# Attention value products of two heads in alternation by key tile, and the second head's probabilities scaled on GpSimd

## The chip, the cores and the metric

The kernel runs on one core of a Trainium2 chip. The time is the device time of one launch, in microseconds; the time of the kernel before is the median of three runs, 3374.5 us.

## The reference, cut to what matters

Two layers over 256 latent tokens and 256 context tokens, 1024 wide, in float32. In each layer an adaLN-modulated RMSNorm and one input projection feed three token mixers; their outputs are gated, merged and projected, and a product-key expert layer (128 picks for each token, gathered from memory) follows. The change lies in the three mixers alone:

```python
# A: 8 query heads on 2 key heads, window of 128, a sink logit;  B: 8 heads, 2-D neighbourhood, bias table
# C: 4 heads of two score maps each (differential attention)
p = softmax(concat([s_loc, s_ctx, sink]))        # A
p = softmax(concat([s + bias, s_ctx]))           # B
a = softmax(s0) - lam * softmax(s1)              # C
o = p @ v
```

Latent tokens read 512 keys (256 latent, 256 context), context tokens read the 256 context keys. The second layer has latent tokens alone.

## The kernel before, in words

The kernel is written with one program for each engine and semaphores between them. The attention of a layer is a list of steps, `STEPS[l]` (L66). A step is one stream `s` (0 latent, 1 context), one unit `u` of two heads (0 to 3 are mixer A, 4 to 7 mixer B, 8 to 11 mixer C) and one tile `qt` of 128 queries: 48 steps in layer 0 (24 latent, then 24 context) and 24 in layer 1 (latent). A latent step of A or B works on two heads (`m` = 0, 1) by 512 keys, a context step on two heads by 256 keys. `a` counts the steps over both layers. Four engines work on neighbouring steps at the same time:

- **TensorE** (`attention`, L675 to L741) goes through scores of step n+2 (L689, L692), transposes of the probabilities of step n (L704: eight 128x128 tiles, four for each head, in PSUM banks 4 and 5), then the value products of step n-1 (L726: for each head one accumulation over four key tiles, head 0 into PSUM partitions 0 to 63 and head 1 into 64 to 127 of one bank). In the float32 type each product is two instructions in the trace.
- **VectorE** (`maxima`, `normalise`, `copy_y`, L1438 to L1496) goes through the mask or bias of step i+1 (L1457), its row maxima (L1458, L1460 to L1462), the sums and reciprocals of step i (L1471, L1472), the scaling of its probabilities (L1475 head 0, L1476 head 1; mixer C has L1478 and L1479 in their place), and the copy of the output of step i-2 (L1486).
- **ScalarE** (L1044 to L1078) takes the exponentials of step i+1 (L1057, L1059) and copies the transposed probabilities of step i out of PSUM (L1071).
- **GpSimd** computes nothing here. It issues the bias tables of mixer B from memory (`biases`, L1236 to L1245), 256 KB for each of the 8 latent steps of B in a layer, into two buffers: table b goes where table b-2 was. The first two of a layer are issued ahead of the attention; table b from the third on waits for `max_ready` of the step that used table b-2, and is thus issued as soon as the row maxima of that step are done:

```python
if b % 8 >= 2:
    back = [k for k, v in BIASED.items() if v == b - 2][0]
    pool.wait_ge(max_ready, back + 1)
```

The order that matters on VectorE is that of L1489 to L1494: `maxima(i + 1)` stands ahead of `normalise(i)`, and its first instruction, L1457, waits for the scores and, in mixer B, for the bias table (L1455). Outside the attention GpSimd issues the gathers of the expert rows, with waits of their own.

Of the kernel before, what the change touches and what calls it, by code (L numbers as in the profile page):

```python
# [12 lines left out]
N_CTX = 256  # L13
T = N_LAT + N_CTX
TT = T // P
DEPTH = 2
# [50 lines left out]
STEP0 = [0, len(STEPS[0])]  # L67
# [105 lines left out]
def build(nc, x_in, small_in, lambda_in, const_in_dram, rope_in, bias_in, stream_in, experts_in, out):  # L173
# [8 lines left out]
    with ctx:  # L182
# [171 lines left out]
        max_ready = sem("max_ready")  # L354
        exp_ready = sem("exp_ready")
        prob_ready = sem("prob_ready")
        probt_done = sem("probt_done")
        probt_copied = sem("probt_copied")
        y_done = sem("y_done")
# [101 lines left out]
        def key_bank(r, n):  # L461

            return 4 + n % 4 if r == 1 else 2 + n % 6

        block = ctx.enter_context(nc.Block())

# [40 lines left out]
        def _(pe):  # L507
# [167 lines left out]
            def attention(l):  # L675
                steps = STEPS[l]

                def scores(n):
                    _, s, u, qt = steps[n]
                    a = STEP0[l] + n  # L680
                    q = UNIT_AT[("abc"[u // 4] + "q", u % 4)]
                    k = UNIT_AT[("abc"[u // 4] + "k", 0 if u < 4 else u % 4)]
                    if n >= 2:
                        pe.wait_ge(exp_ready, a - 1)
                    for m in range(2):
                        rows64 = slice(64 * m, 64 * m + 64)
                        query = feature(l, s, q)[rows64, qt * P:(qt + 1) * P]
                        if l == 0 and s == 0:
                            last = mm(ps[:, 2 * (a % 2) + m, :], query, feat0[rows64, k, :], start=True, stop=True)  # L689
                            continue  # L690
                        for at, ks in enumerate([0, 1] if s == 0 else [1]):
                            last = mm(ps[:, 2 * (a % 2) + m, at * N_LAT:(at + 1) * N_LAT], query,  # L692
                                      feature(l, ks, k)[rows64, :], start=True, stop=True)
                    last.then_inc(scores_done, 1)

                def transposes(n):
                    _, s, u, qt = steps[n]
                    a = STEP0[l] + n
                    pe.wait_ge(prob_ready, a + 1)
                    if a >= 1:  # L700
                        pe.wait_ge(probt_copied, a)
                    for m in range(2 if u < 8 else 1):
                        for t in range(TT if s == 0 else 2):
                            last = nc.tensor.transpose(ps[:, 4 + m, t * P:(t + 1) * P],  # L704
                                                       prob_l[l][:, a % 2, m, t * P:(t + 1) * P], ident)
                    last.then_inc(probt_done, 1)

                def values(n):
                    _, s, u, qt = steps[n]
                    a = STEP0[l] + n  # L710
                    nt = TT if s == 0 else 2
                    pe.wait_ge(probt_copied, a + 1)
                    if a >= 2:
                        pe.wait_ge(y_copied, a - 1)
                    y = ps[:, 6 + a % 2, 0:P]
                    for m in range(2 if u < 8 else 1):
                        for t in range(nt):
                            tile = TT - nt + t
                            if u < 4:
                                v, at = value_tile(l, 0, tile)[:, 64 * m:64 * m + 64], slice(64 * m, 64 * m + 64)  # L720
                            elif u < 8:
                                c0 = 128 * (u - 4) + 64 * m
                                v, at = value_tile(l, 1, tile)[:, c0:c0 + 64], slice(64 * m, 64 * m + 64)
                            else:
                                v, at = value_tile(l, 2, tile)[:, 128 * (u - 8):128 * (u - 7)], slice(0, 128)
                            last = mm(y[at, :], v, probt_l[l][:, a % 2, m, t * P:(t + 1) * P],  # L726
                                      start=(t == 0), stop=(t == nt - 1))
                    last.then_inc(y_done, 1)

                pe.wait_ge(proj_copied, PROJ0[3] if l else PROJ0[1])  # L730
                pe.wait_ge(roped, (l + 1) * len(ROPED))
                pe.wait_ge(v_copied, V0[3] if l else V0[1])
                scores(0)
                scores(1)
                for n in range(len(steps)):
                    if n + 2 < len(steps):
                        scores(n + 2)
                    transposes(n)
                    if n >= 1:
                        values(n - 1)  # L740
                values(len(steps) - 1)  # L741
# [491 lines left out]

        @block.gpsimd
        def _(pool):
            def biases(l):  # L1236
                for a, b in BIASED.items():
                    if (a >= STEP0[1]) != (l == 1):
                        continue
                    if b % 8 >= 2:  # L1240
                        back = [k for k, v in BIASED.items() if v == b - 2][0]
                        pool.wait_ge(max_ready, back + 1)
                    u = b % 8
                    pool.dma_start(bias_l[l][:, b % 2, :, :], bias_in[l, u // 2, u % 2, :, :, :])\  # L1244
                        .then_inc(bias_arrived[b % 2], 16)  # L1245

            def gather(r):
                for n in range(PICKS):
# [14 lines left out]

            pool.wait_ge(mod_cols_copied, 2)
            pool.dma_start(rope_l[0], rope_in).then_inc(rope_in_sem, 16)
            biases(0)
            gather(0)
            gather(1)
            pool.wait_ge(x_ready, 24)
            biases(1)  # L1270
            gather(2)


# [1 line left out]
        def _(dve):  # L1275
# [162 lines left out]
            def attention(l):  # L1438
# [25 lines left out]
                def normalise(i):  # L1464
                    _, s, u, qt = steps[i]
                    a = STEP0[l] + i
                    nk = T if s == 0 else N_CTX
                    st = stat[:, a % 2, :]
                    dve.wait_ge(exp_ready, a + 1)
                    if u < 4:  # L1470
                        link(v.tensor_tensor(st[:, 4:6], st[:, 4:6], st[:, 6:8], ALU.add))  # L1471
                    link(v.reciprocal(st[:, 8:10], st[:, 4:6]))  # L1472
                    p0, p1 = prob[:, a % 2, 0, 0:nk], prob[:, a % 2, 1, 0:nk]
                    if u < 8:
                        v.tensor_scalar(p0, p0, st[:, 8:9], None, ALU.mult)  # L1475
                        v.tensor_scalar(p1, p1, st[:, 9:10], None, ALU.mult).then_inc(prob_ready, 1)  # L1476
                    else:
                        link(v.tensor_scalar(p1, p1, st[:, 9:10], lam[:, 8 + l:9 + l], ALU.mult, ALU.mult))  # L1478
                        v.scalar_tensor_tensor(p0, p0, st[:, 8:9], p1, ALU.mult, ALU.add).then_inc(prob_ready, 1)  # L1479
# [423 lines left out]
```

## Time and profile before

| what | value |
|---|---|
| median of the runs | 3374.5 us (3374.85, 3374.5, 3364.22) |
| the profiled execution, its time | 3379.49 us |
| its span | 3377.7 us |
| mean granted TensorE clock | 0.941 of 2.4 GHz |
| busy in the span: TensorE, VectorE, ScalarE, GpSimd | 82%, 56%, 38%, 25% |
| attention of layer 0, first reciprocal to last | 301.1 to 427.7 us |
| attention of layer 1, first reciprocal to last | 2365.0 to 2442.8 us |

The profiled execution is 5 us longer than the median of the runs. Its span leaves out some 2 us around the first and the last instruction. The busy shares are means over very different stages; the two attention stages are 6% of the span, and only they hold instructions that the change touches. A start of the reciprocal L1472 marks each step once, so its distance from one step to the next is the period of the pipeline.

### The profile page before, as it was taken

The numbers are of one execution on the slowest core, as the hardware profiler recorded it, in microseconds if no ns is written. First come the engines' busy times: TensorE is split into PE (matmuls) and PEld (weight loads), VectorE is DVE, ScalarE is ACT, GpSimd is POOL, SyncE is SP. The second block draws the span as 40 slices with busy tenths as digits, with TensorE's granted clock in tenths as the row PEclk, the third lists the DMA queues.
The fourth block names the chain that finished last, engine by engine and source line by source line (L and its number), as shares of the span: only waits on it lengthen the run. The fifth ranks groups of instructions, "written<-read, shape, count | busy, mean of one in ns | idle before, by whom it ended". The sixth has DMA issues, their size and how long they took to land.

```text
span 3377.7 us, 31495 instructions
## 1 busy us (share of the span) xinstructions
PE 2760.5 (82%) x10860; PEld 1591.4 (47%) x10860; DVE 1881.1 (56%) x3953; ACT 1268.4 (38%) x3289; POOL 838.8 (25%) x790
## 2 busy tenths in 40 slices
PE   6899989984778886877888889888998668778776
PEld 2686668773233553322324455437797622222222
DVE  0336953348833546884555565554854775444444
ACT  1324742231323532333343444334644233333333
POOL 0000000001422322543334444430000044333332
PEclk7899999987988988999999999999998889999999
DMA  7321012224999997999999999993043199999997
GB/s 321 123 88 60 11 50 100 88 100 172 421 421 421 372 358 295 373 422 421 421 421 421 421 403 421 421 410 119 20 150 138 50 382 401 421 422 421 422 421 305
DMA packets 135663, 981.86 MB, mean 291 GB/s; under 512 B 15184, under 2 KB 15312, under 8 KB 16720
## 3 DMA queue, kind: packets, MB, share of 16 engines
q0 software_dynamic: 112032, 810.08, 58.5%
q1 hardware_dynamic: 23184, 167.09, 13.0%
q10 hardware_dynamic: 288, 2.69, 0.2%
q8 instruction: 86, 1.41, 0.2%
q14 instruction: 73, 0.60, 0.0%
HBM read 978.74 MB, written 1.05 MB: 290 GB/s over the span
## 4 chain that ended last, share of the span: by engine, by line
PE 50%; DMA 22%; DVE 17%; ACT 9%; issue 2%; POOL 0%; SPq 0%; ACTq 0%; DVEq 0%
PE ps L874 23%; DMA att<-experts_in,att 19%; PE ps L512 7%; PE ps L513 6%; PE ps L514 6%; DVE att L1687 4%; ACT att L1163 4%; DMA ring<-stream_in 3%; DVE ring_lo L1303 3%; ACT wt_hi L947 2%; PE ps L726 1%; DVE stat L1458 1%; PE ps L544 1%; PE ps L556 1%; DVE att L1575 1%
## 5 line engine op out<-in xcount | busy, mean ns | idle before, releaser
L874 PE MATMUL ps<-att 128*128 128x512 f32 x3072 | 1512.9, 629 | 457.4 <-ACT att L1163 456.5
L1687 DVE CUSTOM_DVE_ANT_0 att<-att 128x1024 f32<-128x1024 f32 x768 | 933.4, 1225 | 756.5 <-DMA att<-experts_in,att 753.4
L1256 POOL DMA_INDIRECT att<-experts_in,att x768 | 828.4, 1079 | 2022.6 <-PE ps L874 1224.3
L874 PEld LDWEIGHTS ps<-att 128*128 128x128 f32 x3072 | 559.6, 196 | 1369.3 <-ACT att L1163 816.5
L1156 ACT ACTIVATE att<-att 128x1 f32<-128x1 f32 x768 | 155.1, 202 | 1086.9 <-DVE att L1687 1077.9
L1303 DVE TENSOR_TENSOR ring_lo<-ring,wt_hi 128x2048 fp32r<-128x2048 f32 x107 | 245.2, 2291 | 395.0 <-ACT wt_hi L947 395.0
L1163 ACT ACTIVATE att<-const,att 128x128 f32<-128x128 f32 x768 | 308.3, 401 | 74.0 <-PE ps L874 3.2
L947 ACT ACTIVATE wt_hi<-ring 128x2048 fp32r<-128x2048 f32 x107 | 204.0, 1907 | 148.5 <-PE ps L514 148.5
L1158 ACT ACTIVATE att<-att 128x1 f32<-128x1 f32 x768 | 226.2, 294 | 24.9
L512 PE MATMUL ps<-h,wt_hi 128*128 128x256 f32 (+1 forms) x576 | 197.8, 343 | 15.5 <-DVE h L1318 14.7
L513 PE MATMUL ps<-h,wt_hi 128*128 128x256 f32 (+1 forms) x576 | 186.8, 324 | 0.0
L514 PE MATMUL ps<-h,ring_lo 128*128 128x256 f32 (+1 forms) x576 | 186.6, 324 | 0.0
L512 PE MATMUL ps<-m,wt_hi 128*128 128x512 f32 (+1 forms) x296 | 114.6, 387 | 20.4 <-DVE m L1318 10.7
L512 PEld LDWEIGHTS ps<-h,wt_hi 128*128 128x128 f32 x576 | 112.5, 195 | 34.4 <-issue 15.1
L513 PEld LDWEIGHTS ps<-h,wt_hi 128*128 128x128 f32 x576 | 113.4, 197 | 11.0 <-issue 3.8
L514 PEld LDWEIGHTS ps<-h,ring_lo 128*128 128x128 f32 x576 | 113.1, 196 | 7.6
L513 PE MATMUL ps<-m,wt_hi 128*128 128x512 f32 (+1 forms) x296 | 111.3, 376 | 0.0
L514 PE MATMUL ps<-m,ring_lo 128*128 128x512 f32 (+1 forms) x296 | 111.2, 376 | 0.0
L512 PE MATMUL ps<-h_lat_hi,wt_hi 128*128 128x256 f32 x360 | 111.1, 309 | 0.0
L533 PE MATMUL ps<-ring,cond 128*32 128x512 f32 x384 | 63.4, 752 | 57.2 <-DMA ring<-stream_in 57.2
L1244 POOL DMA_DIRECT2D att<-bias_in x16 | 8.9, 557 | 376.8 <-DVE stat L1462 352.8
L513 PE MATMUL ps<-h_lat_lo,wt_hi 128*128 128x256 f32 x360 | 102.2, 284 | 0.0
(178 smaller groups left out, 3154.1 us busy)
## 6 DMA issues: line engine op xcount, KB each, us to landing
ring<-stream_in SPq DMA_DIRECT2D x155, 1024.0 KB, 6.1
att<-experts_in,att POOLq DMA_INDIRECT x768, 15.3
att<-bias_in POOLq DMA_DIRECT2D x16, 256.0 KB, 2.9
att<-stream_in SPq DMA_DIRECT2D x3, 1024.0 KB, 7.0
x<-x_in ACTq DMA_DIRECT2D x1, 2048.0 KB, 8.2
out<-att SPq DMA_DIRECT2D x1, 1024.0 KB, 3.9
const<-const_in ACTq DMA_DIRECT2D x1, 576.0 KB, 4.0
att<-rope_in POOLq DMA_DIRECT2D x2, 256.0 KB, 8.2
```

The lines of the kernel that those rows point to most:

```text
L512: mm(dst, a[0], b[0], start=start, stop=False)
L513: mm(dst, a[0], b[1], start=False, stop=False)
L514: return mm(dst, a[1], b[0], start=False, stop=stop)
L533: last = mm(ps[at:at + 32, banks[g % 2], :], cond[:, c, :], ring[:, q % RING, (c % 4) * 512:(c % 4 + 1) * 512], start=(c < 4), stop=(c >= 4))
L874: last = mm(ps[:, d, :], diag[:, m % DIAGS, :], rows[:, m % SLOTS, D + 512 * d:D + 512 * (d + 1)], start=(n % HK == 0), stop=(n % HK == HK ...
L947: nc.scalar.activation(wt_hi[:, d % 2, :], ring[:, DENSE[d] % RING, :], ACT.Copy)\
L1156: nc.scalar.activation(acts[:, n:n + 1], dots[:, n:n + 1], ACT.Gelu).then_inc(gelu_done, 1)
L1158: nc.scalar.activation(acts[:, n:n + 1], acts[:, n:n + 1], ACT.Copy, scale=gates[:, r % 2, n:n + 1])\
L1163: nc.scalar.activation(diag[:, m % DIAGS, :], ident, ACT.Copy, scale=acts[:, n:n + 1])\
L1256: nc.gpsimd.indirect_dma_start(out=rows[:, m % SLOTS, :], out_offset=None, in_=experts_in, in_offset=bass.IndirectOffsetOnAxis(ap=index[:, ...
L1303: v.tensor_tensor(ring_lo[:, DENSE[d] % RING, :], ring[:, DENSE[d] % RING, :], wt_hi[:, d % 2, :], ALU.subtract)\
L1687: v.tensor_tensor_reduce(out=u_row, in0=u_row, in1=h_tok[:, r % 2, n // HK, :], scale=1.0, scalar=0.0, op0=ALU.mult, op1=ALU.add, accum_ou ...
```

## The change

The value products of the two heads alternate: the loop over key tiles is now the outer one, so that head 0 and head 1 take turns. The scaling of head 1 in mixers A and B moves from VectorE to GpSimd; TensorE waits for it ahead of the transposes of head 1 (`second_ready`), and GpSimd waits for the reciprocals (`recip_ready`). The issue of the bias tables is put into the same loop on GpSimd: table b+2 is issued behind the scaling of the step that used table b. Mixer C is as before.

```diff
--- before.py
+++ after.py
@@ -354,6 +354,8 @@
         max_ready = sem("max_ready")
         exp_ready = sem("exp_ready")
         prob_ready = sem("prob_ready")
+        recip_ready = sem("recip_ready")
+        second_ready = sem("second_ready")
         probt_done = sem("probt_done")
         probt_copied = sem("probt_copied")
         y_done = sem("y_done")
@@ -461,6 +463,10 @@
         def key_bank(r, n):
 
             return 4 + n % 4 if r == 1 else 2 + n % 6
+
+        def seconds(a):
+
+            return sum(STEPS[l][n][2] < 8 for l in range(DEPTH) for n in range(len(STEPS[l])) if STEP0[l] + n < a)
 
         block = ctx.enter_context(nc.Block())
 
@@ -700,6 +706,8 @@
                     if a >= 1:
                         pe.wait_ge(probt_copied, a)
                     for m in range(2 if u < 8 else 1):
+                        if m:
+                            pe.wait_ge(second_ready, seconds(a) + 1)
                         for t in range(TT if s == 0 else 2):
                             last = nc.tensor.transpose(ps[:, 4 + m, t * P:(t + 1) * P],
                                                        prob_l[l][:, a % 2, m, t * P:(t + 1) * P], ident)
@@ -713,8 +721,8 @@
                     if a >= 2:
                         pe.wait_ge(y_copied, a - 1)
                     y = ps[:, 6 + a % 2, 0:P]
-                    for m in range(2 if u < 8 else 1):
-                        for t in range(nt):
+                    for t in range(nt):
+                        for m in range(2 if u < 8 else 1):
                             tile = TT - nt + t
                             if u < 4:
                                 v, at = value_tile(l, 0, tile)[:, 64 * m:64 * m + 64], slice(64 * m, 64 * m + 64)
@@ -1233,16 +1241,24 @@
 
         @block.gpsimd
         def _(pool):
-            def biases(l):
-                for a, b in BIASED.items():
-                    if (a >= STEP0[1]) != (l == 1):
-                        continue
-                    if b % 8 >= 2:
-                        back = [k for k, v in BIASED.items() if v == b - 2][0]
-                        pool.wait_ge(max_ready, back + 1)
+            def attention(l):
+
+                def load_bias(b):
                     u = b % 8
                     pool.dma_start(bias_l[l][:, b % 2, :, :], bias_in[l, u // 2, u % 2, :, :, :])\
                         .then_inc(bias_arrived[b % 2], 16)
+
+                for b in (8 * l, 8 * l + 1):
+                    load_bias(b)
+                for n, (_, s, u, qt) in enumerate(STEPS[l]):
+                    a = STEP0[l] + n
+                    if u >= 8:
+                        continue
+                    second = prob_l[l][:, a % 2, 1, 0:T if s == 0 else N_CTX]
+                    pool.wait_ge(recip_ready, a + 1)
+                    nc.gpsimd.tensor_scalar(second, second, stat[:, a % 2, 9:10], None, ALU.mult).then_inc(second_ready, 1)
+                    if a in BIASED and BIASED[a] % 8 < 6:
+                        load_bias(BIASED[a] + 2)
 
             def gather(r):
                 for n in range(PICKS):
@@ -1263,11 +1279,11 @@
 
             pool.wait_ge(mod_cols_copied, 2)
             pool.dma_start(rope_l[0], rope_in).then_inc(rope_in_sem, 16)
-            biases(0)
+            attention(0)
             gather(0)
             gather(1)
             pool.wait_ge(x_ready, 24)
-            biases(1)
+            attention(1)
             gather(2)
 
 
@@ -1469,11 +1485,11 @@
                     dve.wait_ge(exp_ready, a + 1)
                     if u < 4:
                         link(v.tensor_tensor(st[:, 4:6], st[:, 4:6], st[:, 6:8], ALU.add))
-                    link(v.reciprocal(st[:, 8:10], st[:, 4:6]))
+                    v.reciprocal(st[:, 8:10], st[:, 4:6]).then_inc(recip_ready, 1)
+                    dve.wait_ge(recip_ready, a + 1)
                     p0, p1 = prob[:, a % 2, 0, 0:nk], prob[:, a % 2, 1, 0:nk]
                     if u < 8:
-                        v.tensor_scalar(p0, p0, st[:, 8:9], None, ALU.mult)
-                        v.tensor_scalar(p1, p1, st[:, 9:10], None, ALU.mult).then_inc(prob_ready, 1)
+                        v.tensor_scalar(p0, p0, st[:, 8:9], None, ALU.mult).then_inc(prob_ready, 1)
                     else:
                         link(v.tensor_scalar(p1, p1, st[:, 9:10], lam[:, 8 + l:9 + l], ALU.mult, ALU.mult))
                         v.scalar_tensor_tensor(p0, p0, st[:, 8:9], p1, ALU.mult, ALU.add).then_inc(prob_ready, 1)
```

GpSimd in layer 0, from the rope table to the expert gathers, before. A row is one instruction or several like ones; `att` holds the bias tables and the probabilities.

```order
L1265 DMA att<-rope_in 128x512 [waits mod_cols_copied]
L1244 DMA att<-bias_in 128x512 x2
L1244 DMA att<-bias_in 128x512 [waits max_ready] x6
L1256 DMA att<-experts_in,att 128x2048 [waits index_ready,keys_done]
```

The same place now:

```order
L1281 DMA att<-rope_in 128x512 [waits mod_cols_copied]
L1248 DMA att<-bias_in 128x512 x2
L1259 ISA
L1259 TENSOR_SCALAR att<-att,stat 128x512 [waits recip_ready] x9
L1248 DMA att<-bias_in 128x512
L1259 TENSOR_SCALAR att<-att,stat 128x512 [waits recip_ready]
L1248 DMA att<-bias_in 128x512
```

The pair of the last two rows comes six times in a layer. A bias DMA that waited for `max_ready` of its step alone now has no wait of its own and stands behind the scaling of that step, which waits for `recip_ready`. An instruction of the kind ISA stands once ahead of the first scaling.

VectorE around one latent step of mixer B, before (scaling of one step, then the bias and the maxima of the next):

```order
L1472 RECIPROCAL stat<-stat 128x2 [waits exp_ready]
L1475 TENSOR_SCALAR att<-att,stat 128x512 [waits dve_order]
L1476 TENSOR_SCALAR att<-att,stat 128x512
L1486 COPY att<-ps 128x128 [waits y_done]
L1457 TENSOR_TENSOR ps<-ps,att 128x2x256 [waits bias_arrived0,scores_done]
L1458 TENSOR_REDUCE stat<-ps 128x2 [waits dve_order]
```

The same place now:

```order
L1488 RECIPROCAL stat<-stat 128x2 [waits exp_ready]
L1492 TENSOR_SCALAR att<-att,stat 128x512 [waits recip_ready]
L1502 COPY att<-ps 128x128 [waits y_done]
L1473 TENSOR_TENSOR ps<-ps,att 128x2x256 [waits bias_arrived0,scores_done]
L1474 TENSOR_REDUCE stat<-ps 128x2 [waits dve_order]
```

One scaling is gone from VectorE; the wait for the bias table stands where it stood, two instructions behind the scaling of head 0.

## Rows read from the trace of the kernel before

**Rows 1.** The page: span and busy times.

```profile
span 3377.7 us, 31495 instructions
PE 2760.5 (82%) x10860; PEld 1591.4 (47%) x10860; DVE 1881.1 (56%) x3953; ACT 1268.4 (38%) x3289; POOL 838.8 (25%) x790
```

**Rows 2.** Busy time by stretch: PE, PEld, DVE, ACT, POOL, then clock, DMA share, GB/s.

```profile
305.00:327.00 22.00, 21.68 (x166) 14.47 (x163) 20.73 (x57) 15.61 (x37) 0.00 (x0) 0.97 0.00 1
327.00:356.00 29.00, 29.00 (x229) 20.19 (x226) 26.62 (x60) 20.03 (x42) 3.30 (x6) 1.00 0.20 56
```

**Rows 3.** The chain of waits, layer 0, latent steps: start, us, what.

```profile
317.56 0.62 DVE ps L1457
318.20 1.24 DVE stat L1458
...
328.52 1.02 PE ps L704 x8
329.54 1.51 PE ps L726 x16
331.05 1.06 PE ps L689 x4
```

**Rows 4.** VectorE in order of time, one latent step of mixer A.

```profile
316.28 0.17 DVE L1472 RECIPROCAL stat<-stat 128x2 f32<-128x2 f32 x1
316.49 0.48 DVE L1475 TENSOR_SCALAR att<-att,stat 128x512 f32<-128x512 f32 x1
316.89 0.48 DVE L1476 TENSOR_SCALAR att<-att,stat 128x512 f32<-128x512 f32 x1
317.28 0.28 DVE L1486 COPY att<-ps 128x128 f32<-128x128 f32 x1
320.00 0.17 DVE L1472 RECIPROCAL stat<-stat 128x2 f32<-128x2 f32 x1
```

**Rows 5.** VectorE and GpSimd in order of time, one latent step of B.

```profile
330.64 0.16 DVE L1472 RECIPROCAL stat<-stat 128x2 f32<-128x2 f32 x1
331.03 0.54 POOL L1244 DMA_DIRECT2D att<-bias_in  x1 [3.05 <-DVE stat L1462]
332.16 0.70 DVE L1457 TENSOR_TENSOR ps<-ps,att 128x512 f32<-128x512 f32 x1 [0.18 <-PE ps L689]
334.15 0.17 DVE L1462 TENSOR_SCALAR stat<-stat 128x2 f32<-128x2 f32 x1
334.23 0.16 DVE L1472 RECIPROCAL stat<-stat 128x2 f32<-128x2 f32 x1
334.62 0.54 POOL L1244 DMA_DIRECT2D att<-bias_in  x1 [3.05 <-DVE stat L1462]
```

**Rows 6.** The chain of waits, layer 0, context steps.

```profile
389.97 0.26 DVE att L1476
...
396.84 0.66 PE ps L704 x4
397.49 0.59 PE ps L726 x8
398.09 0.63 PE ps L692 x4
```

**Rows 7.** Bias DMAs: all; those within layer 0's attention; landing of the latter.

```profile
L1244 POOL DMA_DIRECT2D att<-bias_in x16: 538/538/613, 103.6 to 2409.1; - x16
...
L1244 POOL DMA_DIRECT2D att<-bias_in x6: 538/538/613, 327.4 to 345.4; - x6
DMA to landing us min/median/max: 2.8/2.9/3.1
```

**Rows 8.** L1476 at 328 to 352 us: min/median/max ns.

```profile
L1476 DVE TENSOR_SCALAR att<-att,stat x7: 480/555/556, 327.8 to 349.2; 128x512 f32<-128x512 f32 x7
```

**Rows 9.** Other operations on 512 or 1024 elements a partition, same engines' lines.

```profile
L1479 DVE SCALAR_TENSOR_TENSOR att<-att,stat x24: 483/750/752, 359.4 to 2443.5; 128x512 f32<-128x512 f32 x16, 128x256 f32<-128x256 f32 x8
L1458 DVE TENSOR_REDUCE stat<-ps 128x2 f32<-128x1024 f32 x11 | 13.5, 1225 | 0.4
```

## The prediction, made before the changed kernel had run

> **What bounds the kernel now.** I read the page first [rows 1]: TensorE is the busiest engine, but its 82% is a mean over stages, and the change touches the attention alone. So I cut the two attention stages into stretches [rows 2]. In the latent steps of mixer A (305 to 327 us) both TensorE and VectorE are busy nearly all the time; in those of mixer B (327 to 356 us) TensorE is busy without a break and VectorE has 2.4 us free in 29. GpSimd does nothing but six short issues. The chain of waits then says which of the two sets the pace [rows 3]: in mixer A it runs along VectorE's own order, in mixer B along TensorE's: 1.02 transposes + 1.51 value products + 1.06 scores = 3.59 us a step. The reciprocals give the periods: in A 320.00 - 316.28 = 3.72 us [rows 4], in B 334.23 - 330.64 = 3.59 us [rows 5]. VectorE in B waits only 0.18 us for the scores, so both engines are near their limit and a gain needs both to get shorter. In B the bias table never makes anyone wait: it is issued at 331.03, 2.9 us later it is there [rows 5, 7], at some 333.9, and the L1457 that needs it comes one step after 332.16, at 335.75.
>
> **The change, part by part.** *Scaling of head 1 off VectorE.* L1476 and what follows stand 317.28 - 316.89 = 0.39 us apart [rows 4], call it 0.40. In a latent A step VectorE then needs 3.72 - 0.40 = 3.32 us. In a context step the piece on the chain is 0.26 us [rows 6].
>
> *Value products in alternation.* For 16 instructions TensorE takes 1.51 us [rows 3], for the 8 of a context step 0.59 us [rows 6]. Both contain some 0.2 us of changeover, so the work is 1.31 and 0.39 us: twice the instructions take 3.4 times as long. The two heads write different halves of the partitions; in the short case the second head's products evidently run beside the first's, in the long case only partly, because the second head comes too late in the order. If alternation makes the long case like the short one, it takes 2 x 0.39 + 0.05 + 0.2 = 1.03 us, a saving of 0.48 us. TensorE's sum in a latent step falls from 3.59 to 3.11 us. The context steps save nothing, they are overlapped already.
>
> *What these two bring.* Latent A: 8 steps in each layer, now 3.32 us, bound by VectorE: 16 x 0.40 = 6.4 us. Context A: 8 x 0.26 = 2.1 us. In context B TensorE alone needs 0.66 + 0.59 + 0.63 us a step [rows 6] and none of it shrinks, so I count nothing. Of the latent B steps some three in each layer at the ends of the stretch gain about 0.45 us: 6 x 0.45 = 2.7 us. Together -11.2 us.
>
> *The bias tables, the step that decides.* Until now table b+2 was issued when the maxima of the step of table b were done. Now it stands on GpSimd's queue behind the scaling of that step, which needs its reciprocal. But VectorE computes `maxima(i + 1)` ahead of `normalise(i)`: the reciprocal of step a comes a full step after its maxima, and behind it only the scaling of head 0 (0.40) and the copy (0.20) stand between VectorE and the L1457 of step a+2, which needs table b+2. The table is thus wanted 0.8 us after the start of the reciprocal, and cannot be issued earlier than that. VectorE stops; behind the stopped L1457 stand the maxima, the next reciprocal, hence GpSimd's next scaling and the next table. The six tables that are not loaded ahead in a layer form a chain of their own, one table a step. Its period, from reciprocal to reciprocal:
>
> - reciprocal 0.16 us [rows 5];
> - its release of GpSimd, 0.30 us: L1462 ends at 334.32, GpSimd starts at 334.62 [rows 5];
> - the scaling on GpSimd. No row has GpSimd computing. The nearest below is the same operation on VectorE, 0.48 us [rows 4]; above, a pass over twice the elements on VectorE, 1.22 us [rows 9]. I take 0.80, a little above the 0.75 of the two-input operation on the same tile [rows 9], since I see no reason for GpSimd to be quicker than VectorE's slower forms;
> - issue to landing 2.9 us [rows 7], and 0.1 us to release VectorE;
> - L1457 to the reciprocal, 334.23 - 332.16 = 2.07 us [rows 5].
>
> Sum 0.16 + 0.30 + 0.80 + 2.9 + 0.1 + 2.07 = 6.33 us, against 3.59 now: +2.74 us, twelve times (six in each layer) = **+32.9 us**. TensorE has some 3 us of free time in each of these periods, so its saving is worth nothing there.
>
> *Late transposes of head 1.* Head 0's scaling starts 0.21 us after the reciprocal and takes 0.48 [rows 4]; with a short release and half of the transposes (0.51) TensorE comes to head 1 some 1.25 us after the reciprocal starts. GpSimd is done at 0.16 + 0.30 + 0.80 = 1.26: just covered. If it can't work beside VectorE's scaling it starts at 0.74 and is done at 1.54, 0.29 late, on every second step since TensorE's result is used two steps on. I count 2 us over all the A steps. That the two disturb each other is seen already: L1476 takes 0.555 us where a GpSimd issue falls on it [rows 8] and 0.48 us in mixer A, where none does [rows 4].
>
> The Trainium skill, "SBUF — State Buffer", section "Who interferes with whom", says more: the port pair that both use is an exclusive lock, held for a whole instruction by whichever came first, and the other blocks. By that rule the sum depends on who is first; VectorE first is the 0.29 us above, GpSimd first is a rival below. The Trainium skill's "GPSIMD Engine Reference", section "Engine selection", calls one-input operations there roughly line-rate, by its 128 lanes at 1.2 GHz an estimate of 0.43 us for 512 elements; by that the sum below would be near +17 us. No row here can show either.
>
> *The ISA instruction* ahead of GpSimd's first scaling stands right behind the first two tables, which were issued from 103.6 us on [rows 7]; the first reciprocal comes at 301.1 us (the table of the profile), which covers it. *The clock*: 0.97 to 1.00 in these stages [rows 2]. With TensorE at half load in the B stretch it may fall to 1.2 GHz there; doubled, TensorE's 3.11 us would be 6.2 and still fit a period of 6.3. I count nothing.
>
> **Sum:** -11.2 + 32.9 + 2 = +23.7, say +24 us. On the profiled execution's own time, 3379.5, that is 3403.5; that execution stood 5 us above the median, so on the median I predict 3374.5 + 24 = **3398.5 us**. A difference of 0.3% (10 us) is about what a measurement of this kernel can tell from none.
>
> Bounds: GpSimd at 0.48 us and released in 0.04: period 5.75, 12 x 2.16 = 25.9, less 11.2 = +15, 3389 us. GpSimd at 1.22 us and starting at 0.74: period 0.74 + 1.22 + 0.1 + 2.9 + 2.07 = 7.03, 12 x 3.44 = 41.3, late transposes some 8, less 11.2 = +38, 3413 us.
>
> **The rivals.**
>
> *The multiply is taken first (12%).* GpSimd starts ahead of head 0's scaling and holds it up for its whole 0.8 us. The A steps then need 3.32 + 0.8 = 4.1 us on VectorE, 0.4 more than now rather than 0.4 less: 16 x 0.8 = 13 us above my sum, and some 5 us in the context steps: +42, 3416 us. For it: both are released by the same semaphore. Against it: GpSimd needed 0.30 us where VectorE's own next instruction comes after 0.04.
>
> *The table is issued before the multiply ends (8%), no measurable change.* If GpSimd passes on to the DMA while its scaling is still running, the 0.80 drops out: period 5.53, 12 x 1.94 = 23.3, and at a landing of 2.8 us 22; less 11.2 and a few tenths more at the short end, +9: 3383 us. Against it: GpSimd's program is one queue, and no row shows it at two things at once.
>
> *The transfer stays hidden, faster (6%).* Then B gains its 0.48 too: -(16 x 0.40 + 16 x 0.48 + 2.1) = -16, 3358 us. It decides where the table lands within 0.8 us of the reciprocal's start; the balance point, at which the stalls eat the 11.2 us exactly, is 0.93 us a step, a period of 4.5 us or a landing about 1 us after issue. All six of layer 0's landings took 2.8 to 3.1 us [rows 7], so only a wrong reading of the order would bring this about.
>
> *The alternation gives nothing (beside these).* TensorE then keeps 3.59 us, the A steps gain 0.13 rather than 0.40: 16 x 0.27 = 4 us worse, 3403 us, inside my range.
>
> **How the numbers follow.** My case has 74%, GpSimd first 12%, no change 8%, faster 6%. My case and GpSimd first are slower by more than 0.3%: slower 0.86, same 0.08, faster 0.06. The range takes in my case with its bounds (3389 to 3413), the edge of the second (3416) and, for the spread of the runs, reaches down to 3384.
>
> **What would show it.** Right: in the B stretches L1473 (now the bias instruction) waits some 2.7 to 3.5 us for a bias DMA six times a layer, reciprocals 5.8 to 7 us apart; latent A periods near 3.3 us; 16 value instructions in about 1.0 us; GpSimd's scaling between 0.5 and 1.2 us. Wrong: B periods at or under 3.6 us, or A periods above 3.7 us.

## The result, and the profile after

The changed kernel takes **3418.4 us** (median of 4 runs, 3417.7 to 3422.9) against 3373.8 us (4 runs, 3364.2 to 3374.9): a ratio of 1.014, interval 1.0125 to 1.0156. It is slower by 44.6 us. (The ratios here and below stand with their 95% intervals; they are not the quotients of the medians, from which they can differ by 0.1%.) The forecast was 3398.5 us with a range up to 3416: the sign was right, the cost nearly twice as large. The profiled execution took 3422.9 us. Its page, against [rows 1]:

```profile
span 3421.0 us, 31497 instructions
...
PE 2772.0 (81%) x10860; PEld 1588.1 (46%) x10860; DVE 1865.5 (55%) x3905; ACT 1267.3 (37%) x3289; POOL 915.3 (27%) x838
```

VectorE lost 48 instructions but only 15.6 us of busy time; GpSimd gained the 48 and 76.5 us. The stretches, against [rows 2] (the second and third are the B stretches of layers 0 and 1):

```profile
305.00:328.00 23.00, 20.87 (x178) 12.62 (x180) 19.59 (x54) 15.13 (x36) 11.14 (x6) 1.00 0.00 1
328.00:378.00 50.00, 34.01 (x210) 20.92 (x206) 19.91 (x44) 18.58 (x39) 18.00 (x14) 0.76 0.12 32
2418.00:2466.00 48.00, 31.60 (x228) 22.67 (x226) 19.57 (x42) 17.63 (x37) 17.92 (x14) 0.79 0.12 34
```

No engine is busy for 70% of the B stretch: its pace is set by waits. The chain of waits there, from one GpSimd scaling to the next (start, us, what), answers to the B half of [rows 3]:

```profile
351.25 1.79 POOL att L1259
353.04 2.96 DMA att<-bias_in
...
356.10 0.71 DVE ps L1473
...
356.83 1.24 DVE stat L1474
...
358.09 0.17 DVE stat L1478
358.26 0.08 DVE stat L1488
...
358.44 1.80 POOL att L1259
```

This is the forecast chain: scaling, table, bias add, maxima, reciprocal, scaling. Its period is 7.19 us where 6.33 was forecast, and the term that stands out is GpSimd's 1.80. The waits at 328 to 378 us (reader <- releaser: us in total, count, longest) agree; VectorE's five waits for a table are 4.6 us each on average:

```profile
POOL att L1259 <- DVE stat L1488: 32.3, 8, 6.3
DVE ps L1473 <- DMA att<-bias_in: 23.2, 5, 5.7
```

In mixer A VectorE's own order no longer makes the chain, as it did in [rows 3]:

```profile
310.45 1.87 POOL att L1259
...
312.37 0.66 PE ps L712 x4
313.02 1.02 PE ps L734 x16
314.05 1.08 PE ps L695 x4
...
315.15 0.71 DVE ps L1473
...
315.89 1.24 DVE stat L1474
...
317.68 0.18 DVE stat L1488
...
317.94 1.87 POOL att L1259
```

One round trip here is 317.94 - 310.45 = 7.49 us and covers two steps: TensorE waits for GpSimd ahead of head 1's transposes, and what it then computes is used two steps on. The periods alternate between 3.35 and 4.14 us, a mean of 3.74 against 3.72 before. The forecast had named A periods above 3.7 us as a sign of being wrong, and this sign was there.

The growth, cut by the start of each reciprocal, both layers together, beside the forecast's terms:

| stretch of the attention | before, us | after, us | change | forecast |
|---|---|---|---|---|
| A, latent (8 periods a layer) | 58.9 | 58.4 | -0.5 | -4.4 |
| B with late tables (6 a layer) | 43.2 | 89.0 | +45.8 | +32.9 |
| B, last step of the stretch | 5.7 | 4.2 | -1.5 | -2.7 |
| the two steps after it | 14.4 | 18.7 | +4.3 | 0 |
| other latent steps | 37.3 | 37.0 | -0.4 | 0 |
| context steps | 44.8 | 46.4 | +1.6 | -2.1 |
| sum | 204.3 | 253.7 | +49.3 | +23.7 |

Outside the attention the profiled span is 6.0 us shorter, in three pieces of at most 2.9 us that touch no changed line; the runs of before alone spread over 10 us, so I read nothing into it.

### The profile page after: what moved, and what is told of

It is laid out like the page before. It is cut to its first block, busy times and chain, and to the rows that moved or that the text cites. A ratio compares the mean times of both kernels' runs of the same rounds, so it can differ in the third digit from the quotient of the medians.

```text
span 3421.0 us, 31497 instructions
## 1 busy us (share of the span) xinstructions
PE 2772.0 (81%) x10860; PEld 1588.1 (46%) x10860; DVE 1865.5 (55%) x3905; ACT 1267.3 (37%) x3289; POOL 915.3 (27%) x838
## 3 DMA queue, kind: packets, MB, share of 16 engines
HBM read 978.74 MB, written 1.05 MB: 286 GB/s over the span
## 4 chain that ended last, share of the span: by engine, by line
PE 47%; DMA 24%; DVE 17%; ACT 8%; issue 2%; POOL 2%; SPq 0%; ACTq 0%; DVEq 0%
PE ps L882 23%; DMA att<-experts_in,att 20%; PE ps L518 6%; PE ps L519 6%; PE ps L520 6%; DVE att L1703 4%; ACT att L1171 3%; DMA ring<-stream_in 3%; DVE ring_lo L1319 3%; ACT wt_hi L955 2%; DVE stat L1474 2%; POOL att L1259 1%; DMA att<-bias_in 1%; PE ps L550 1%; DVE att L1591 1%
## 5 line engine op out<-in xcount | busy, mean ns | idle before, releaser
L1259 POOL TENSOR_SCALAR att<-att,stat 128x512 f32<-128x512 f32 (+1 forms) x48 | 76.6, 1596 | 403.4 <-DVE stat L1488 403.4
L518 PEld LDWEIGHTS ps<-h,wt_hi 128*128 128x128 f32 x576 | 112.4, 195 | 33.2 <-issue 14.4
L712 PE MATMUL ps<-const,att 128*128 128x128 f32 x400 | 75.0, 314 | 50.6 <-DVE att L1492 24.9
```

What stands on the lines that cost most here:

```text
L518: mm(dst, a[0], b[0], start=start, stop=False)
L1259: nc.gpsimd.tensor_scalar(second, second, stat[:, a % 2, 9:10], None, ALU.mult).then_inc(second_ready, 1)
```

## The experiments

Two theories at the start. *Mine*: the chain reciprocal, scaling, table, bias add makes the loss, and GpSimd's slow scaling lengthens it. *Rival*: the slow scaling itself makes it, through TensorE's wait for head 1 and through VectorE being disturbed, and the place of the table matters little.

**1. The tables early again.** The change as it is, but each table issued once the maxima of its step are done, ahead of the wait for the reciprocal:

```diff
+ if a + 1 in BIASED and BIASED[a + 1] % 8 < 6:
+     pool.wait_ge(max_ready, a + 2)
+     load_bias(BIASED[a + 1] + 2)
  pool.wait_ge(recip_ready, a + 1)
  nc.gpsimd.tensor_scalar(second, ...)
- if a in BIASED and BIASED[a] % 8 < 6:
-     load_bias(BIASED[a] + 2)
```

> The changed kernel, but each bias table is issued as in the kernel before: when the maxima of the step that used table b-2 are done, ahead of GpSimd's wait for the next reciprocal. My theory (the late tables cost most): the twelve periods of about 7.1 us in mixer B fall to 3.4 to 4.4 us, no DMA wait at the bias instruction, and the time falls from 3418 to about 3377 us (3 us above the kernel before, since GpSimd's 1.85 us scaling still holds up the transposes of head 1). Rival 1 (the slow GpSimd scaling alone costs the 45 us, the tables were only late because of it): the time stays above 3400 us. Rival 2 (GpSimd's issues of the tables come late because the scaling of 1.85 us fills its queue): DMA waits of over 0.5 us remain.

Measured 3372.3 us, ratio 1.0004 (0.9995 to 1.0013). No bias DMA makes VectorE wait, and the window shows TensorE near full again:

```profile
328.00:356.00 28.00, 25.89 (x224) 15.68 (x220) 21.33 (x46) 18.71 (x40) 15.42 (x12) 1.00 0.18 48
```

So with the tables early nearly nothing of the loss is left in the time of the kernel. But the periods in B are now 3.30 and 4.20 us in turn, in A 3.31 and 4.18: the two gains that the forecast counted are eaten by something.

**2. The alternation alone**, on the kernel before:

```diff
- for m in range(2 if u < 8 else 1):
-     for t in range(nt):
+ for t in range(nt):
+     for m in range(2 if u < 8 else 1):
```

> The kernel before with the alternation of the value products alone. My theory: 16 value instructions in about 1.03 us in place of 1.51; mixer A stays at 3.72 us a step (VectorE bound), mixer B goes from 3.59 to about 3.27 us; in all -7 us, 3366 us. Rival (the alternation is worth nothing, or its gain is eaten by the clock): B stays at 3.59, 3373 us. Rival (the first step's order on TensorE is all that counts): -15 us or more.

Measured 3363.0 us, 0.9975 (0.9965 to 0.9985): faster. Periods are 3.71 us in A and 3.32 in B, and the chain in B has moved from TensorE to VectorE:

```profile
331.98 0.61 DVE ps L1457
...
332.62 1.24 DVE stat L1458
...
334.55 0.56 DVE att L1476
```

The first experiment, measured beside it, differs by the scaling on GpSimd and its signals, and took 9.4 us more. The scaling on GpSimd is a loss even where the tables are early.

**3. The tables late alone**: experiment 2, which has both scalings on VectorE, with the tables behind the reciprocal in place of the maxima (the reciprocal signals `recip_ready` as in the change):

```diff
- pool.wait_ge(max_ready, back + 1)
+ pool.wait_ge(recip_ready, back + 1)
```

> Alternation as changed, both scalings on VectorE, GpSimd computes nothing, but each table waits for the reciprocal rather than for the maxima of the step that used table b-2. My theory: the late wait alone makes the chain: periods of 0.16 + 0.1 to 0.3 + 3.0 + 0.1 + 2.07 = 5.4 to 5.6 us for twelve steps (7.1 less GpSimd's scaling), in all +18 us against the kernel before, 3391 us, and more if the clock falls. Rival (without the scaling in the queue the tables come in time): B periods under 4 us and a time at or under 3374 us.

Measured 3396.8 us, 1.0068 (1.0051 to 1.0085), so +33.8 us on experiment 2. VectorE in order of time:

```profile
337.39 0.70 DVE L1458 TENSOR_TENSOR ps<-ps,att 128x512 f32<-128x512 f32 x1 [2.31 <-DMA att<-bias_in]
339.46 0.16 DVE L1473 RECIPROCAL stat<-stat 128x2 f32<-128x2 f32 x1
343.13 0.70 DVE L1458 TENSOR_TENSOR ps<-ps,att 128x512 f32<-128x512 f32 x1 [2.40 <-DMA att<-bias_in]
345.20 0.16 DVE L1473 RECIPROCAL stat<-stat 128x2 f32<-128x2 f32 x1
```

A period is 5.74 us with no GpSimd arithmetic in the kernel at all. The chain is the wait's doing; the rival falls. The time is 6 us above the 3391 expected: the periods are a little longer than 5.6 us, and the first step behind each stretch takes 4.79 and 4.76 us where experiment 2 has 3.17 and 3.20.

**4. The scaling alone**: experiment 1 with the two loops of experiment 2 turned back.

> Head 1 scaled on GpSimd, tables issued early, value products in the old order. My theory: GpSimd takes 1.85 us, TensorE waits about 0.8 us for it on every second step; latent steps of A and B near 4.0 us on average against 3.72 and 3.59, in all +11 us against the kernel before, 3385 us. Rival (the scaling is covered by TensorE's other work and VectorE gains 0.40 us): -5 us or better.

Measured 3384.9 us, 1.004 (1.0024 to 1.0055). Periods 3.60 and 4.38 us in both mixers. Beside experiment 1 (3372.3) the alternation is worth 12.6 us; on the kernel before it was worth 8.2. The change is thus three parts that partly cancel: the alternation gains 8 us, the scaling on GpSimd then costs 9, and the place of the tables costs the remaining 43 to 46.

**5. GpSimd behind head 0's scaling**: experiment 1, but the two engines no longer scale at the same time.

```diff
- pool.wait_ge(recip_ready, a + 1)
+ pool.wait_ge(prob_ready, a + 1)
```

> As the run with the tables early, but GpSimd starts its scaling only when VectorE has finished that of head 0 (it waits for prob_ready rather than recip_ready), so the two never overlap. If VectorE's scaling holds a port that GpSimd needs (rival), GpSimd's scaling, no longer blocked, takes about 0.4 us less in the trace, 1.4 us, and the time is the same as with the tables early, 3372 us. If the two do not disturb each other (my theory, since both show their usual durations side by side), GpSimd still takes 1.85 us, is done 0.5 us later, the two-step period of mixer A grows from 7.5 to about 8 us, and the time is about 8 us longer than with the tables early, 3380 us.

Measured 3376.6 us, 1.002 (1.001 to 1.0029). Of GpSimd's scaling the line view (min/median/max ns) says

```profile
L1262 POOL TENSOR_SCALAR att<-att,stat x48: 922/1565/1582, 299.9 to 2421.2; 128x512 f32<-128x512 f32 x32, 128x256 f32<-128x256 f32 x16
```

where the changed kernel, with VectorE's scaling beside it, has

```profile
L1259 POOL TENSOR_SCALAR att<-att,stat x48: 1082/1844/1867, 299.1 to 2464.0; 128x512 f32<-128x512 f32 x32, 128x256 f32<-128x256 f32 x16
```

Apart from VectorE's scaling it takes 1.56 us for 512 elements and 0.92 for 256. So the two do disturb each other, against what I expected: the overlap costs GpSimd 0.28 us. Starting later costs more than that: A goes to 3.32 and 4.40 us.

**6. Only half of head 1 on GpSimd**: experiment 1, VectorE scales head 0 and the first half of head 1's keys.

```diff
- second = prob_l[l][:, a % 2, 1, 0:T if s == 0 else N_CTX]
+ nk = T if s == 0 else N_CTX
+ second = prob_l[l][:, a % 2, 1, nk // 2:nk]
...
- v.tensor_scalar(p0, p0, st[:, 8:9], None, ALU.mult).then_inc(prob_ready, 1)
+ part = prob[:, a % 2, 1, 0:nk // 2]
+ v.tensor_scalar(p0, p0, st[:, 8:9], None, ALU.mult)
+ v.tensor_scalar(part, part, st[:, 9:10], None, ALU.mult).then_inc(prob_ready, 1)
```

> As the run with the tables early, but GpSimd scales only the second half of head 1's keys and VectorE the first half. My theory: GpSimd takes 1.08 us for 256 elements (and about 0.7 for 128), which TensorE hardly waits for; VectorE gets 0.27 us back, so mixer A takes about 3.6 us a step without the alternation of 3.3 and 4.2; against the kernel before -9 us, 3362 us. Rival (GpSimd costs by the instruction, not by the element): no change against the run with the tables early, 3372 us.

Measured 3368.4 us, 0.9993 (0.9984 to 1.0002): no clear gain, where 3362 was expected. Periods 3.80 us in A, 3.36 to 3.53 in B. One step of A in order of time:

```profile
313.25 0.49 DVE L1495 TENSOR_SCALAR att<-att,stat 128x512 f32<-128x512 f32 x1
313.30 1.22 POOL L1263 TENSOR_SCALAR att<-att,stat 128x256 f32<-128x256 f32 x1 [2.58 <-DVE stat L1490]
313.65 0.57 DVE L1496 TENSOR_SCALAR att<-att,stat 128x256 f32<-128x256 f32 x1
```

VectorE's second scaling has 256 elements and takes 0.57 us; the line view of the kernel before has that shape in the context steps, with no GpSimd work beside it:

```profile
L1475 DVE TENSOR_SCALAR att<-att,stat x6: 352/354/354, 385.3 to 396.2; 128x256 f32<-128x256 f32 x6
```

Each slows the other, and what VectorE gives away it gets back in part as longer instructions of its own.

**7. What VectorE can give to ScalarE instead.** Experiment 2 showed VectorE as the bound. Here, on top of experiment 2, ScalarE makes the output copies out of PSUM, between `exps(i + 1)` and `copy_probt(i)`, and VectorE no longer makes them; both scalings stay on VectorE. The added lines:

```diff
+ act.wait_ge(y_done, a + 1)
+ nc.scalar.activation(yt_l[l][:, u, t0:t0 + P], ps[:, 6 + a % 2, 0:P], ACT.Copy).then_inc(y_copied, 1)
```

> The alternation alone, with the copies of the outputs out of PSUM moved from VectorE to ScalarE, which waits 0.8 us a step for TensorE. My theory: VectorE's 0.20 us leaves the steps of mixer A (3.71 to 3.51 us) and of the context steps; against the kernel before -12 us, 3359 us. Rival (ScalarE's exponentials come later, and its copy of the transposed probabilities with them): no better than the alternation alone, 3363 us, or worse.

Measured 3354.5 us, 0.9963 (0.995 to 0.9977); A 3.51 us, B 3.25.

**8. Does the clock cost anything?** The changed kernel, with six unread products of 128x256 ahead of the value products of the second to the seventh of the eight B steps of a layer (steps 9 to 14), to keep TensorE busier there:

```diff
+ if BIASED.get(a, 0) % 8 in range(1, 7):
+     for _ in range(6):
+         mm(ps[:, 6 + a % 2, 256:512], ident, const[:, 0:256], start=True, stop=True)
```

> The changed kernel with six products of 256 columns whose results nobody reads, ahead of the value products in the steps of mixer B that stall. They keep TensorE busy in the stalls. If the clock's fall costs time there and behind (my theory), the granted clock in 328 to 378 us goes from 0.76 to near 1.0, the first steps of mixer C lose their 6.5 and 5.5 us periods (to about 4.2), and the time falls by about 4 us to 3414. Rival (the clock costs nothing, a period of 7.1 us hides it): the same time, 3418, or more by the filler's own.

Measured 3421.3 us, 1.0156 (1.0142 to 1.017). The clock of the stretch rose from 0.76 to 0.86 only, and the first step after it got no shorter (6.76 us). My reading, not tried apart: the filler began too late and stood in the way at the end. It does not answer the question; experiment 12 is the second attempt.

**9. The table ahead of the scaling**, both still behind the wait for the reciprocal (the changed kernel with two statements exchanged).

```diff
+ if a in BIASED and BIASED[a] % 8 < 6:
+     load_bias(BIASED[a] + 2)
  nc.gpsimd.tensor_scalar(second, ...)
- if a in BIASED and BIASED[a] % 8 < 6:
-     load_bias(BIASED[a] + 2)
```

> The changed kernel, but each table is issued on GpSimd ahead of the scaling of its step, still behind the wait for the reciprocal. My theory (the chain of the late tables is reciprocal, scaling 1.85, transfer, maxima): the scaling drops out of it, the twelve periods go from about 7.15 to about 5.6 us, VectorE still waits some 2.3 us for each table; the time goes down by 12 x 1.5 = 18 us from 3418 to about 3400 us. Rival (the scaling behind the issue sits in the same queue and is now late for TensorE, which takes the gain back): periods above 6.5 us, a time above 3410 us.

Measured 3397.7 us, 1.0073 (1.0058 to 1.0089), some 23 us better than the change by the ratios. The chain of waits no longer holds GpSimd's arithmetic:

```profile
346.45 2.84 DMA att<-bias_in
...
349.38 0.71 DVE ps L1473
...
350.12 1.24 DVE stat L1474
...
351.62 0.29 issue
351.91 2.92 DMA att<-bias_in
```

The period is 5.5 us. This splits the change's 7.15 us: 1.65 come from standing behind the scaling (its 1.80 less 0.19 by which GpSimd's release is shorter, 0.10 against the 0.29 of "issue" here), 1.9 (5.5 - 3.59) from standing behind the reciprocal.

**10. Two signals, both scalings on VectorE**: experiment 7, and TensorE may transpose head 0 as soon as head 0 is scaled.

```diff
  for m in range(2 if u < 8 else 1):
+     if m:
+         pe.wait_ge(second_ready, seconds(a) + 1)
...
- v.tensor_scalar(p0, p0, st[:, 8:9], None, ALU.mult)
- v.tensor_scalar(p1, p1, st[:, 9:10], None, ALU.mult).then_inc(prob_ready, 1)
+ v.tensor_scalar(p0, p0, st[:, 8:9], None, ALU.mult).then_inc(prob_ready, 1)
+ v.tensor_scalar(p1, p1, st[:, 9:10], None, ALU.mult).then_inc(second_ready, 1)
```

> Alternation, output copies on ScalarE, both scalings on VectorE, and TensorE waits for head 0 and head 1 apart, as in the changed kernel. My theory: the steps of mixer B, which a loop over two steps between VectorE and TensorE holds at 3.25 us, come down to about 3.15 us; A stays at 3.51 us, bound by VectorE; 2 us better than without, 17 us below the kernel before. Rival (nothing waits there): the same time as without.

Measured **3350.1 us**, 0.9929 (0.9914 to 0.9944): the best here, faster than both kernels. In B TensorE has no free time left, and its three parts start 1.03, 1.02 and 1.06 us apart:

```profile
328.00:353.00 25.00, 25.00 (x224) 15.63 (x222) 23.28 (x49) 21.34 (x51) 2.14 (x4) 1.00 0.14 43
```

```profile
331.12 0.16 DVE L1490 RECIPROCAL stat<-stat 128x2 f32<-128x2 f32 x1
331.88 1.09 PE L711 MATMUL ps<-const,att 128*128 128x128 f32 x8
332.91 1.09 PE L733 MATMUL ps<-att 128*64 128x128 f32 x16
333.93 1.13 PE L694 MATMUL ps<-att 64*128 64x512 f32 x4
334.24 0.16 DVE L1490 RECIPROCAL stat<-stat 128x2 f32<-128x2 f32 x1
...
334.99 1.10 PE L711 MATMUL ps<-const,att 128*128 128x128 f32 x8
```

The period, 3.12 us, is TensorE's 3.11 of the forecast.

**11. Experiment 7 once more**, beside experiment 10.

> The alternation with the output copies on ScalarE once more, beside the run with two signals on the same chip. My theory: 15 us below the kernel before again (ratio 0.9955). Rival (the first measurement was a lucky one): only 8 us, as with the alternation alone.

Measured 3356.9 us, 0.9957 (0.9944 to 0.9971): the gain of experiment 7 is there again, and the two signals are worth 6.8 us more by the medians. In the profiled executions the attention of the two layers is 3.0 us shorter with them (187.0 against 190.0); the rest lies outside what they touch, so the 3 us are shown and the 6.8 are not explained.

**12. The filler two steps earlier**, with the value products of steps 7 (the last of A) to 12 of a layer rather than 9 to 14; the edit is against experiment 8.

```diff
- if BIASED.get(a, 0) % 8 in range(1, 7):
+ if a in range(STEP0[l] + 7, STEP0[l] + 13):
```

> The filler products of the earlier run, moved to where TensorE's idle time begins (value products of steps 7 to 12 of a layer rather than 9 to 14), so that none stands in the way when the stalls end. If the clock's fall is what lengthens the end of the stretch (my theory), the granted clock in 328 to 378 us is above 0.95, the first step of mixer C takes about 4.2 us in place of 6.5 and 5.5, and the time is 3 to 4 us below the changed kernel's: ratio to the kernel before 1.012 to 1.013. Rival (the end of the stretch is long for another reason): the clock at 1.0 and the step still 5.5 us or more.

Measured 3417.7 us, 1.0137 (1.012 to 1.0154). The windows of experiment 12 and, below it, of experiment 8:

```profile
328.00:378.00 50.00, 41.21 (x289) 28.20 (x286) 20.48 (x45) 19.16 (x40) 18.01 (x14) 1.00 0.12 33
```

```profile
328.00:378.00 50.00, 41.36 (x264) 28.24 (x264) 20.13 (x45) 19.52 (x40) 18.00 (x14) 0.86 0.12 32
```

The clock now stays at 1.00 (2.4 GHz), and the normal periods of the chain remain 7.1 to 7.25 us: inside the chain the slow clock cost nothing. The first step after it takes 4.17 and 4.19 us in the two layers where the change had 6.46 and 5.53. Over the two steps behind each stretch that is 4.1 us, which is nearly all of the +4.3 in the table. The kernel's own time does not resolve this (44.8 us over the kernel before, where the change has 44.6). In the profiled execution the attention is 2.8 us shorter than the change's (250.9 against 253.7), with four slow landings (below) rather than three.

## Why the prediction was right, and where it was wrong

**The chain: right.** One table a step, through scaling, DMA, bias add, maxima and reciprocal. Experiments 1, 3 and 9 show it from three sides. These terms held: reciprocal, landing 2.9 us, 2.07 from the bias add to the reciprocal. The release of GpSimd was over-counted: 0.26 us from the reciprocal's start to GpSimd's, where 0.16 + 0.30 was taken, 12 x 0.2 = -2.4 us.

**The scaling on GpSimd: the step that failed.** Forecast 0.80 us, with 1.22 as the upper bound; in order of time the change shows

```profile
343.83 0.16 DVE L1488 RECIPROCAL stat<-stat 128x2 f32<-128x2 f32 x1
344.03 0.48 DVE L1492 TENSOR_SCALAR att<-att,stat 128x512 f32<-128x512 f32 x1
344.10 1.84 POOL L1259 TENSOR_SCALAR att<-att,stat 128x512 f32<-128x512 f32 x1 [6.33 <-DVE stat L1488]
```

1.85 us against 0.80: 12 x 1.05 = +12.6 us, about as much as the 12.9 by which the B term was short (the release and the slow landings below leave 1.0 us, and 0.7 us of smaller differences go against it). The bound was taken from rows of VectorE, and "no reason for GpSimd to be quicker than VectorE's slower forms" says nothing of how much slower it can be: three to four times VectorE's 0.48 us. With no row of GpSimd computing, the upper end should have stood much further out.

The Trainium skill, "GPSIMD Engine Reference", section "Engine selection", calls one-input operations there roughly line-rate, by the estimate in the forecast 0.43 us for 512 elements; the runs don't agree: 1.56 us apart from VectorE's scaling.

**Slow landings, +3.4 us, not foreseen.** Three of the twelve tables landed after 3.6 to 4.5 us rather than 2.9 (periods 8.70, 7.83 and 8.28 us instead of about 7.15). The DMA view of one of them, 336 to 342 us (queue: packets, MB, share; then the transfer and its landing in us):

```profile
q0 software_dynamic: 80, 0.26, 17.9%
q8 instruction: 1, 0.02, 1.8%
...
att<-bias_in POOLq DMA_DIRECT2D x1, 256.0 KB, 4.5
```

and of a normal one, 344 to 350 us:

```profile
q0 software_dynamic: 80, 0.26, 16.4%
...
att<-bias_in POOLq DMA_DIRECT2D x1, 256.0 KB, 2.9
```

In the slow one a 16 KB packet of queue 8, of the kind "instruction", came in at the same time, and so it did in the other two. Such a packet alone does not make a landing slow: what differs is when it comes. All fourteen traces of this case together have 168 tables issued inside the attention. In ten of them a packet of queue 8 began 0.9 to 1.8 us after the issue, and all ten landed late, after 3.6 to 4.5 us; the 97 with no packet of the two instruction queues landed after 2.7 to 3.2 us. When that packet began before 0.2 us or from 2.2 us on, the landing took at most 3.3 us, but for one of 3.7; and with an 8 KB packet of queue 14, the other of that kind, and none of queue 8 it took at most 3.6. That the one causes the other was not tried.

**The gain in A: right as far as VectorE goes, wrong in the sum.** VectorE alone can do a step in 3.3 us (the short ones of each pair). "Just covered" was the wrong reading: GpSimd is done 0.26 + 1.85 = 2.11 us after the reciprocal's start, and TensorE wanted it at 1.25. The trace has three such waits in the A steps of each layer, 0.77 us idle each, like this one:

```profile
312.37 0.66 PE L712 MATMUL ps<-const,att 128*128 128x128 f32 x4 [0.77 <-POOL att L1259]
```

Each makes a period some 0.85 us longer: 3 x 0.85 x 2 layers = 5.1 us where 2 were counted. And the first period of A in each layer (3.85 and 3.87 us) is the same with and without the change, so that 14 periods gain the 0.40 us and not 16, another 0.8 us. With these -6.4 becomes -0.5, which is what the table has. In the context steps the same wait (periods 2.44 and 1.92 in A, 2.09 and 1.81 in B) turned -2.1 into +1.6.

**The clock: "I count nothing" was right inside the chain and wrong at its end.** The stretches ran at 0.76 and 0.79, in turn at 1.2 and 2.4 GHz. Behind the last table TensorE was the bound again, still at the low level (0.50 from 374.5 to 381 us, 1.00 behind it): the 4.1 us of experiment 12.

**The alternation: right.** 16 value instructions took 1.02 us (forecast 1.03), and the 8 of a context step 0.59 us as before. Its worth, 8.2 us by experiment 2, is limited by VectorE; in B experiment 10 takes that limit away too.

**The rivals.** "The multiply is taken first": no, head 0's scaling starts first and keeps its 0.48 us in the rows above. "The table is issued before the multiply ends": no, the scaling of 351.25 ends at 353.04 and the DMA begins there. "The transfer stays hidden": only experiment 1, which moves the wait, hides it.

The sum, step by step: +12.9 in the late-table chain (12.6 scaling, 3.4 landings, -2.4 release, -0.7 the rest), +3.9 in A, +3.7 in the context steps, +4.3 behind the stretch and +0.8 elsewhere are 25.6 us more than forecast in the attention; the 6.0 us outside it stand against them.

## What to carry to other kernels

When arithmetic goes to an engine that also issues loads, look first at what is queued behind it: moving the issue back ahead of the new wait recovered 43 to 46 us, and no speed of the scaling would have (experiment 3 has no scaling on GpSimd and still loses 34 us to the wait). Before an engine that the trace never shows computing is given work, price it far above its neighbour's figure and ask who waits for it one and two steps on. Work can instead be taken from the bound by giving a waiting engine its input in two parts, or by a copy on an engine that has time: together with the alternation these made the kernel 0.7% faster.

## What the runs showed of the hardware

- GpSimd multiplies 128x512 fp32 by a scalar a partition in 1.56 us and 128x256 in 0.92 us, with VectorE's scaling not beside it. A line through the two sizes is 2.5 ns an element of a partition and 0.28 us beside it. Beside VectorE's scaling it is 1.85 and 1.08 us.
- The two engines slow each other, but neither is shut out. In experiment 6 GpSimd's scaling ran from 313.30 to 314.52 us, and VectorE began and ended a scaling within it, in 0.57 us rather than 0.35. The Trainium skill, "SBUF — State Buffer", section "Who interferes with whom", describes an exclusive lock on the port pair that the two share when VectorE is in a 2-port mode, held for a whole instruction by whichever issued first. The rows of experiment 6 don't agree with that, as far as GpSimd's spans can be trusted, which the profile calls rough: the second scaling neither kept its 0.35 us nor waited for GpSimd's end. Which mode VectorE was in no run here shows.
- TensorE's 16 value instructions (8 products) took 1.51 us head by head and 1.02 us in alternation: the same instructions on two halves of the output partitions, 0.49 us for their order alone. With 8 instructions it was 0.59 us in both orders.
